# A two-kind transformer stack on one core: the second block's attention rearranged

## The reference

```python
def gqa_block(q):          # 8 heads of 64, keys of 2 heads
    sc = jnp.einsum('bqkgd,blkd->bkgql', qg, ka).astype(jnp.float32) * scale
    p = jax.nn.softmax(sc, axis=-1).astype(va.dtype)
    o = jnp.einsum('bkgql,blkd->bqkgd', p, va)
...
def diff_block(q):         # 4 heads, each of two score maps
    sc = jnp.einsum('bqhjd,blhjd->bhjql', q, kb).astype(jnp.float32) * scale
    p = jax.nn.softmax(sc, axis=-1)
    w = (p[:, :, 0] - lam * p[:, :, 1]).astype(vb.dtype)
    o = jnp.einsum('bhql,blhe->bqhe', w, vb)
    o = rms_norm(o, subln_g) * (1.0 - lam_init)
...
mixed = jnp.concatenate([out_a, out_b], axis=-1)
x = x + jnp.einsum('ble,ed->bld', mixed, w_out[l])
```

## Time and profile before

| | |
|---|---|
| median of 3 runs | 2423.42 us (2422.56 to 2423.81) |
| profiled execution | 2427.16 us, of it a span of 2425.4 us |
| busy, share of the span | PE 95%, PEld 76%, DVE 44%, ACT 25%, POOL 61% |
| the chain that ended last | PE 82%, DVE 11%, ACT 3% |
| attention loop of the second block | about 1856 to 2013 us of the span |
| PE busy in 2080 to 2425 us | 342.21 of 345.00 us |

### The profile page before, as it was taken

How to read it: one execution, slowest core, us unless ns; L and a number is a source line. 1 busy time by engine, 2 the same in 40 slices (tenths; PEclk the granted TensorE clock), 3 DMA queues, 4 the chain that set the end, 5 groups by cost and what they waited for, 6 DMA issues and landing times.

```text
span 2425.4 us, 30534 instructions
## 1 busy us (share of the span) xinstructions
PE 2307.5 (95%) x10971; PEld 1851.8 (76%) x10971; DVE 1069.5 (44%) x1623; ACT 608.6 (25%) x1058; POOL 1478.2 (61%) x1452
## 2 busy tenths in 40 slices
PE   5989999999999999898999999999998879999999
PEld 4666888888888887677878888888976436788887
DVE  7894663543331158858635322311482552423200
ACT  3324323321110023243232211110232451211100
POOL 5664745677766766546547767667492216777763
PEclk9999999999999998998999999999999989999999
DMA  3321222422223333212334222223331002222232
GB/s 143 103 70 59 86 91 81 163 96 96 96 100 98 96 103 96 70 53 74 92 102 152 96 95 95 95 88 99 114 114 45 1 0 70 87 95 95 96 101 81
DMA packets 68628, 217.35 MB, mean 90 GB/s; under 512 B 8368, under 2 KB 8496, under 8 KB 68400
## 3 DMA queue, kind: packets, MB, share of 16 engines
q1 hardware_dynamic: 52640, 187.72, 23.9%
q10 hardware_dynamic: 15888, 28.21, 3.3%
HBM read 195.93 MB, written 10.49 MB: 85 GB/s over the span
## 4 chain that ended last, share of the span: by engine, by line
PE 82%; DVE 11%; ACT 3%; issue 1%; POOL 1%; DMA 1%; ACTq 0%; SPq 0%; POOLq 0%; DVEq 0%
PE ps L1540 71%; PE ps L1815 2%; DVE score L1333 2%; PE ps L1973 2%; DVE small L1329 2%; ACT pe L939 2%; PE ps L1725 1%; PE ps L1746 1%; DVE small L1214 1%; DVE rt L1295 1%; POOL w_lo L504 1%; PE ps L1761 1%; DVE rt L1288 1%; DVE b_sb L1390 1%; PE ps L2022 1%
## 5 line engine op out<-in xcount | busy, mean ns | idle before, releaser
L504 POOL TENSOR_TENSOR w_lo<-w_raw,w_hi 128x512 fp32r<-128x512 f32 x700 | 959.3, 1370 | 58.4
L501 POOL TENSOR_SCALAR w_hi<-w_raw 128x512 fp32r<-128x512 f32 x700 | 497.6, 711 | 728.7 <-DMA w_raw<-wst 684.2
L1540 PE MATMUL ps<-h_hi,w_lo 128*128 128x512 f32 (+1 forms) x2048 | 807.1, 394 | 25.4 <-POOL w_lo L504 12.8
L1540 PE MATMUL ps<-h_lo,w_hi 128*128 128x512 f32 (+1 forms) x2048 | 789.5, 385 | 0.0
L1540 PE MATMUL ps<-h_hi,w_hi 128*128 128x512 f32 (+1 forms) x2048 | 788.3, 385 | 0.0
L1540 PEld LDWEIGHTS ps<-h_hi,w_lo 128*128 128x128 f32 x2048 | 390.3, 191 | 124.2 <-POOL w_lo L504 26.4
L1540 PEld LDWEIGHTS ps<-h_lo,w_hi 128*128 128x128 f32 x2048 | 390.7, 191 | 79.1 <-issue 6.2
L1540 PEld LDWEIGHTS ps<-h_hi,w_hi 128*128 128x128 f32 x2048 | 390.4, 191 | 76.8
L1540 PE MATMUL ps<-a_hi,w_lo 128*128 128x512 f32 (+1 forms) x572 | 214.4, 375 | 0.0
L1540 PE MATMUL ps<-a_hi,w_hi 128*128 128x512 f32 (+1 forms) x572 | 213.9, 374 | 0.0
L1540 PE MATMUL ps<-a_lo,w_hi 128*128 128x512 f32 (+1 forms) x572 | 213.7, 374 | 0.0
(11 more groups left out here) (277 smaller groups left out, 2639.5 us busy)
## 6 DMA issues: line engine op xcount, KB each, us to landing
w_raw<-wst SPq DMA_DIRECT2D x350, 512.0 KB, 3.5
rot<-raw ACTq DMA_DIRECT2D x70, 128.0 KB, 2.1
gates<-gt ACTq DMA_DIRECT2D x32, 256.0 KB, 4.1
stage<-gates ACTq DMA_DIRECT2D x32, 256.0 KB, 4.0
x_sb<-xin SPq DMA_DIRECT2D x4, 512.0 KB, 7.9
out<-x_sb SPq DMA_DIRECT2D x8, 256.0 KB, 4.4
kc<-cst ACTq DMA_DIRECT2D x1, 1056.0 KB, 4.9
kc<-cst ACTq DMA_DIRECT2D x1, 481.0 KB, 5.0
```

Source lines behind the costliest of these rows:

```text
L501: eng.tensor_scalar(w_hi[s][:, part], w_raw[s][:, part], 1.0, 1.0, ALU.mult, ALU.mult)\
L504: eng.tensor_tensor(w_lo[s][:, part], w_raw[s][:, part], w_hi[s][:, part].bitcast(F32), ALU.subtract)\
L1540: m = eng.matmul(o, w, x, start=first and i == 0, stop=final and i == 2)
```

## The change

All of it is in the second block's attention.

- The scores against the meta tokens are made once, for all 32 steps, as 64 products of 16 columns behind the scores of steps 0 and 1, into banks 6 and 7. VectorE copies them to `m_sb` and takes their negated maxima (`nmeta`). In each step VectorE then takes the smaller of the two negated maxima, adds it to the meta scores (`meta_cols`), ScalarE makes one more exponential of 128 x 32, and VectorE adds its sums to the others.
- Score tiles alternate between banks 0, 1 and banks 2, 3. Scores of step t wait for the exponentials of step t-2. `LAG` is 4.
- ScalarE evicts transposes ahead of the step's exponentials (not in b0), and evicts all of them in differential units. VectorE's `difference` runs two steps behind. A differential result is squared from PSUM, and scaled from PSUM.
- `values` is in two parts, with the next step's scores between them.
- GpSimd splits half a chunk of output weights (`wo2` to `wo5`) behind the multiplications of steps 1, 3, ... 15.
- The first slices of the output tiles stand between the last transposes.

```diff
-LAG = 2
+LAG = 4
...
-        def score_tile(u, i):
-            at = 0 if i == 0 else 1024 - META + 512 if u < PAIRS_A else 1024
-            return ps[:, at:at + TM]
+        def score_tile(t, i):
+            return bank(2 * (t % 2) + i)
...
+                        if b % 2:
+                            h = t // 2
+                            w = index[(L2, "wo2")] + h // 2
+                            if h % 2 == 0:
+                                eng.wait_ge(w_dma[w % WSLOTS], 16 * (w // WSLOTS + 1))
+                                eng.sem_inc(w_seen, 1)
+                            split_half(w, w % WSLOTS, h % 2)
...
-            done = between
+            done = between + 4
...
+                eng.wait_ge(nm2_ready, t + 1)
                 for i in range(2):
-                    s, col = 2 * t + i, 8 * (u % 2) + 2 * b + i
-                    eng.wait_ge(nm2_ready, s + 1)
-                    eng.activation(pe[u % 2][:, 2 * b + i, :], score_tile(u, i), ACT.Exp,
+                    col, at = 8 * (u % 2) + 2 * b + i, META * i if u < PAIRS_A else 0
+                    eng.activation(pe[u % 2][:, 2 * b + i, at:at + T], score_tile(t, i), ACT.Exp,
                                    bias=small[:, col:col + 1], accum_out=small[:, 16 + col:17 + col])\
                        .then_inc(e2_ready, 1)
+                eng.wait_ge(md2_ready, t + 1)
+                eng.activation(meta_cols(t), meta_cols(t), ACT.Exp).then_inc(em2_ready, 1)
...
-                h = u - PAIRS_A
-                if h:
-                    eng.wait_ge(ysp_lo, 8 * L2 + 4 + h)
-                eng.activation(osb2[:, :], bank(7), ACT.Copy).then_inc(y2_taken, 1)
-                eng.wait_ge(y2_taken, h + 1)
-                eng.activation(osq2[:, :], osb2[:, :], ACT.Square).then_inc(osq2_ready, 1)
+                eng.activation(osq2[:, :], bank(7), ACT.Square).then_inc(osq2_ready, 1)
...
             for t in range(STEPS + LAG + TB):
+                u, b = divmod(t - LAG, TB)
+                turn = 0 <= t - LAG < STEPS
+                if turn and b:
+                    turned(t - LAG)
                 if t < STEPS:
                     exps(t)
-                u, b = divmod(t - LAG, TB)
-                if b == 0 and u:
+                if b == 0 and u > 0:
                     result(u - 1)
+                if turn and b == 0:
+                    turned(t - LAG)
                 if b == 1 and u > PAIRS_A:
                     result_norm(u - 1 - PAIRS_A)
                 if b == 2 and u > PAIRS_A:
                     result_split(u - 1 - PAIRS_A)
-                if 0 <= t - LAG < STEPS:
-                    turned(t - LAG)
-                    if b == TB - 1:
-                        turned_meta(u)
+                if turn and b == TB - 1:
+                    turned_meta(u)
...
+            def meta_scores():
+                eng.wait_ge(mk2_ready, 1)
+                for i in range(2):
+                    eng.tensor_copy(m_sb[:, i, :], bank(6 + i)).then_inc(mk2_taken, 1)
+                eng.wait_ge(mk2_taken, 2)
+                for i in range(2):
+                    k = step(eng.tensor_reduce(nmeta[:, i:64:2], m_sb[:, i, :].rearrange("p (t m) -> p t m", m=META),
+                                               AX.X, ALU.max, negate=True))
+                after(k)
...
+            def raw_maxima(t):
+                at = 80 + 2 * (t % 2)
+                for i in range(2):
+                    eng.wait_ge(s2_ready, 2 * t + i + 1)
+                    k = step(eng.tensor_reduce(small[:, at + i:at + i + 1], score_tile(t, i), AX.X, ALU.max, negate=True))
+                return k
...
+                col, at = 8 * (u % 2) + 2 * b, 80 + 2 * (t % 2)
+                eng.tensor_tensor(small[:, col:col + 2], small[:, at:at + 2], nmeta[:, 2 * t:2 * t + 2], ALU.min)\
+                   .then_inc(nm2_ready, 1)
+                eng.wait_ge(nm2_ready, t + 1)
+                if u >= 2 and b == 0:
+                    eng.wait_ge(tm_ready, u - 1)
+                less = small[:, col:col + 2].rearrange("p (i o) -> p i o", o=1).to_broadcast([P, 2, META])
+                eng.tensor_tensor(meta_cols(t), m_sb[:, :, META * t:META * (t + 1)], less, ALU.add).then_inc(md2_ready, 1)
...
+                after(step(eng.tensor_reduce(small[:, at:at + 2], meta_cols(t), AX.X, ALU.add)))
+                after(step(eng.tensor_tensor(small[:, 16 + c:18 + c], small[:, 16 + c:18 + c], small[:, at:at + 2], ALU.add)))
...
+            raw_maxima(0)
+            raw_maxima(1)
+            meta_scores()
             for t in range(STEPS + LAG + TB):
+                if t < STEPS:
+                    if t >= 2:
+                        after(raw_maxima(t))
+                    maxima(t)
                 if 0 < t <= STEPS:
                     inverse_sums(t - 1)
-                if t < STEPS:
-                    maxima(t)
-                if 0 < t <= STEPS:
-                    difference(t - 1)
+                if 1 < t <= STEPS + 1:
+                    difference(t - 2)
...
+                if t < 2:
+                    for i in range(2):
+                        taken(eng, (L2, f"vb{2 * t + i}"))
+                else:
+                    eng.wait_ge(e2_ready, 2 * t - 2)
+                for i in range(2):
+                    rows = slice(64 * i, 64 * i + 64)
+                    eng.matmul(score_tile(t, i), qab[rows, u, b * P:(b + 1) * P], kab[rows, keys_of(u), 0:T],
+                               start=True, stop=True).then_inc(s2_ready, 1)
...
+            def meta_scores():
+                taken(eng, (L2, "vbm"))
+                for t in range(STEPS):
+                    u, b = divmod(t, TB)
                     for i in range(2):
                         rows = slice(64 * i, 64 * i + 64)
-                        metas_first = i == 1 and u < PAIRS_A
-                        at = part.start if not metas_first else 0 if part.start else META
-                        o = score_tile(u, i)[:, at:at + part.stop - part.start]
-                        m = eng.matmul(o, qab[rows, u, b * P:(b + 1) * P], kab[rows, keys, part], start=True, stop=True)
-                        if part.start:
-                            m.then_inc(s2_ready, 1)
+                        m = eng.matmul(bank(6 + i, META * t, META), qab[rows, u, b * P:(b + 1) * P],
+                                       kab[rows, keys_of(u), T:TM], start=True, stop=True)
+                m.then_inc(mk2_ready, 1)
...
+                        eng.wait_ge(yb_ready, u - PAIRS_A)
...
+            def first_outputs(ks):
+                if ks[0] == 0:
+                    eng.wait_ge(e2_ready, 2 * STEPS)
+                cs = [chunk((L2, f"wo{i}")) for i in range(4)]
+                for k in ks:
+                    eng.wait_ge(ysp_lo, 8 * L2 + k + 1)
+                    for i in range(4):
+                        m = product(bank(i), *weights(cs[i], k), h_hi[:, k, :], h_lo[:, k, :], k == 0, k == KT - 1)
+                        if k == KT - 1:
+                            m.then_inc(w_used, 1)
+            scores_2(0)
+            scores_2(1)
+            meta_scores()
             for t in range(STEPS + LAG + 1):
-                if t < STEPS:
+                u, b = divmod(t - LAG, TB)
+                if 2 <= t < STEPS and (b != 1 or u <= 0):
...
+                if t > STEPS:
+                    first_outputs(range(t - STEPS - 1, t - STEPS))
+                if b == 0 and u > 0:
+                    values(u - 1, (0, 1))
+                    if t + 1 < STEPS:
+                        scores_2(t + 1)
+                    values(u - 1, (2, 3))
...
+            first_outputs(range(LAG, KT - 1))
+            o_square_2(HH - 1)
+            first_outputs(range(KT - 1, KT))
```

More of the change, by code:

```diff
@@ L495, in _, with split_half @@
             rounds = len(chunks) // WSLOTS
+            def split_half(c, s, i):
+                part = slice(512 * i, 512 * (i + 1))
+                eng.tensor_scalar(w_hi[s][:, part], w_raw[s][:, part], 1.0, 1.0, ALU.mult, ALU.mult)\
+                   .then_inc(w_top, 1)
+                eng.wait_ge(w_top, c * 2 + (i + 1))
+                eng.tensor_tensor(w_lo[s][:, part], w_raw[s][:, part], w_hi[s][:, part].bitcast(F32), ALU.subtract)\
+                   .then_inc(w_ready, 1)
             def split(c, s, landed):
```

123 lines of the change are left out of this document (55 added, 68 removed).

## The result

The changed kernel takes 2438.32 us (median of 4 runs, 2432.25 to 2440.94) where the kernel before takes 2423.27 (4 runs): ratio 1.0061, 95% interval 1.0047 to 1.0074. A second measurement of the same kernel gave 2434.68 against 2424.41: ratio 1.0048 (1.0035 to 1.0062). So it costs 10 to 15 us; the forecast was 5.7.

A forecast was written before the change was run, and what follows sets the result against it. The prediction took the attention loop as bound by a ring of latencies, the rest by unchanged products. Terms -0.4 - 1.9 + 0.5 + 8.8 - 7.3 + 4.5 + 1.5 = +5.7 on 2423.42 gave 2429 us, range 2415 to 2439 (8 in 10).

The forecast's parts named there:

- Two score tiles, plain units: Plain units of the loop: VectorE's step of 2.75 us replaces the 3.6 us ring; three units change by -0.4 us.
- The place without overlap: Plain units: VectorE's split of the result waits for values ahead of the next reductions, idle some 4 us.
- Unit 3 to 4: Loop from unit 3's values to unit 4's: 16.3 us against 18.16, a change of -1.9 us.
- Differential units: Units 4 to 6 of the loop: two units take 38.8 us against 38.3 at full clock, +0.5 us.
- The start: Loop start: first exponentials wait for all meta scores, taken as 7.7 us; +8.8 us, +12.6 with clock and lock terms.
- The rival at 0.23 a pass: Loop start: meta scores run at 0.23 us a pass, 7 us more, 2436 us in all; chance 0.14.
- The end: From unit 6's values: output slices fill gaps, with a bare 3.6 us wait ahead of the last; -7.3 us.
- Half chunks: GpSimd's weight splits moved into the loop: the 16 operations gain nothing, since TensorE never waited for them.
- GpSimd beside VectorE: Loop: half chunks hold VectorE's small two-input operations; 0.25 us in plain units, +1.5 at the start, between 0 and +4.
- What the clock does: Loop: stretches at 1.2 GHz cost 2.3 us at the start, 2.2 in differential units; +4.5, bounds 0 and +9.
- throughput decides: Rival, whole loop: a unit takes what its fullest engine takes; 2400 us, or 2414 for half of it; chance 0.15.
- clock and locks cost nothing: Rival, whole loop: low clock and GpSimd's holds on VectorE add nothing; 2423 us; chance 0.2.

The follow-up runs named there:

- e3: The changed kernel with VectorE's next-step reductions moved ahead of its waits for a unit's result or norm: 2428.4 us, ratio 1.0015 to the kernel before.
- e6: The changed kernel with a unit's values in one part again, the next step's scores behind them: 2432.8 us, ratio 1.0043 to the kernel before.
- e8: The changed kernel with 2, 4 and 7 unused products filling TensorE's idle ahead of values of units 4, 5, 6: 2432.4 us, ratio 1.0034 to the kernel before.
- e5: The kernel before with only the early output slices, laid into the drain behind the last scores: 2416.5 us, ratio 0.9969 to the kernel before.
- e1: The changed kernel measured again, nothing altered: 2434.7 us, ratio 1.0048 to the kernel before.
- e7: The changed kernel with meta scores in two parts, only steps 0 to 7 ahead of the first exponentials: 2430.0 us, ratio 1.0025 to the kernel before.
- e4: The changed kernel with GpSimd splitting nothing inside the loop, wo2 to wo5 split behind it: 2438.5 us, ratio 1.0065 to the kernel before.
- e12: The changed kernel with whole values, two-part meta scores, filled gaps, early reductions in differential units, last sum of squares earlier: 2408.4 us, ratio 0.9934 to the kernel before.
- e2: The changed kernel with meta scores made inside the value projection, ahead of its third weight chunk: 2435.6 us, ratio 1.0051 to the kernel before.
- e11: The kernel before with early output slices plus three unused products ahead of scores in steps 20 to 30: 2418.4 us, ratio 0.9978 to the kernel before.

## Why the prediction came out as it did

The sign, the range (2415 to 2439 holds 2438.32, barely) and the list of pieces were right; the size, 5.7 us, was 0.4 to 0.55 of the 15.0 and 10.3 measured. Terms went wrong both ways, and the range held by its width. Step by step:

- **Two score tiles, plain units.** Right. VectorE's step is 2.69 us (2.75 forecast), the idle ahead of the result's split 4.55 (about 4), the unit 17.02 (17.4). The place without overlap is real: e3 takes 0.7 out of it, e6 takes the 0.96 of scores out. The forecast had those 0.96 in its sum and read them as a term; it did not say that this part of the change works against the others. It does. Three plain units gained 1.0 in after's first profile and lost 0.7 in its second (53.27 against 52.60).
- **Unit 3 to 4.** Right: -1.7 against -1.9.
- **Differential units.** The working at full clock was near: 38.8 forecast, 39.43 in e8, of which a part is its own fill. "About as empty as before" was wrong. TensorE idles 14.1 us of units 4 to 6 where it idled 9.4, in three pieces of up to 7.51 us, the largest ahead of the values, where the longest piece before was 3.03. The values then run at half speed on the chain. The 2.2 that I took for it were 1.8 to 3.8, 3.1 from the mean (e8 against the five). But the base was lucky: before's units took 38.36 at clock 0.93, and 40.10 at 0.84 in e5. So the loss against before is 4.9 in the table and, from the means (42.5 and 39.2), 3.3. e3 adds that the order of VectorE was worth 2 to 4 us in two units; I had counted it as given.
- **The start.** +13.5 here, +12.6 forecast, but five executions with this start (after, e1, e3, e6, e8) took 65.08 to 68.67, mean 66.7, so the fair figure is +15.2. The step that failed first is the price of the meta stream: 10.13 instead of 7.7, past the 9 us that the prediction itself named as a sign of being wrong. L1617 was a fair row for the full clock (the first 68 records of the stream took 3.88 us, 0.114 a pair), but inside the stream the clock fell. The rival at 0.23 a pass is half true: 0.158 on average, over the 0.15 from which it was to decide, and 0.213 from start to start once the clock is low. e7 shows what its place on the path is worth, 4.4 us or more.
- **The end.** The order and the bare wait came out as forecast (3.70 against 3.6), the sum did not: -4.5 against -7.3. Unit 6's values took 5.44 for 3.63, and the 108 products behind the gap 26.17 us, where 96 take 22.00 at clock 1.00: 1.4 too long. Both are the clock again, and their 3.2 us are all of the missing 2.8.
- **Half chunks.** "Gain nothing" was wrong. Without them (e4) the end is some 5 us longer, since slices of four tiles need all four split when the drain begins. I had looked at whether TensorE waited for them in the old order, and not in the new one.
- **GpSimd beside VectorE.** The hold is there (1.02 for 0.16 beside L514, as in the earlier trace rows) and costs nothing in the plain units: e4 takes it away and they are 0.05 to 0.07 shorter, so the 0.25 was too much. At the start the 1.5 was rather too little. Three held additions and a held L1259 (0.58 for 0.19) stand on after's chain there, 3.1 us over their quiet times, and without half chunks (e4) the way from the first exponential to unit 0's values is 2.0 us shorter than in after, and further below the four others. The lock of the Trainium skill ("SBUF — State Buffer", on the two separate sides) agrees with these rows.
- **What the clock does.** This is the mis-sized term: +4.5 with an upper bound of 9. By pieces: 1.8 to 3.8 in units 4 to 6; 1.8 + 1.4 at the end, which I had given nothing; 2.4 in the meta stream, and by execution up to 3.6 more in the start. Together 7.4 to 9.4 and upward, 1.6 to 2.1 times the term, and at its bound or beyond. The start of before repeats within 0.2 us (51.57, 51.47, 51.39 in three profiles); that of after varies by 3.6 with the same instructions. In e1, the longest, TensorE's clock is low for 23.9 us between the first scores and unit 0's values, in after for 20.5.

Of the rivals, "throughput decides" and "clock and locks cost nothing" are out. The slow meta stream's 2436 is nearest to what was measured, but only 2.4 of its 7 us came from the stream. e12 gives "throughput decides" its due: the gain was in the design, 17 us under before, once order and clock let it through.

What stays open: why what comes ahead of the loop varies by up to 15 us in unchanged code; and what two parts of the change, evictions ahead of exponentials and differences two steps behind, and the fourth step of lag are worth by themselves. None of them was run apart.

## What to carry to other kernels

When several steps are put in flight, ask where the idle time of TensorE will be gathered and what stands behind it: here products of the chain ran at 1.2 GHz behind gaps of 2.4 to 7.5 us. That it costs more than idle time in smaller pieces is not shown; before's code, with no gap over 3.03 us in these units, had a clock of 0.84 there in e5. Splitting a long group of products to let other work through pays only if somebody waits for that other work ahead of the group's result. And look at the order of a late-joining queue (here GpSimd's splits) against the new order of its consumer, not the old.

## What the hardware showed beyond that

- The clock fell inside a stream in which TensorE was 96% busy: from 1852 to 1862 it is busy 9.63 us of 10, with 16-column products, at clock 0.65, and it is 0.50 behind it. The same stream in e2 left thirteen wide products behind it at half speed. With 512-column products, busy for 14.00 of 14.00 us, the clock was 1.00 throughout (1835 to 1849).

```profile
1835.00:1849.00 14.00, 14.00 (x63) 10.26 (x62) 0.00 (x0) 2.39 (x4) 0.00 (x0) 1.00 0.22 75
1852.00:1862.00 10.00, 9.63 (x118) 9.53 (x116) 1.50 (x3) 0.00 (x0) 0.00 (x0) 0.65 0.07 26
```

- Products whose result nobody uses shortened a chain by 1.8 to 3.8 us (e8), and lengthened another, where they filled all of the idle time (e11).
- VectorE's addition of 128 x 2 was held to 1.02 us beside GpSimd's L514 and lengthened the plain unit by 0.07 us at most; at the start of the loop three such holds stood on the chain of waits.
